# Turning layer 0's memory-head softmax weights: TensorE transposes replaced by VectorE block transposes

## The chip, the cores and the metric

The kernel runs on one core of a Trainium2 chip. The metric is the device time of the program in microseconds (us). The engines named below are TensorE (PE; its weight loads are PEld), VectorE (DVE), ScalarE (ACT), GpSimd (POOL) and SyncE (SP, which issues the DMAs).

## The reference, cut to what matters

A trunk of two decoder layers over 256 tokens of width 2048. Layer 0 mixes tokens by stick-breaking attention, layer 1 by sparse attention; in both, four more heads attend to 256 memory tokens:

```python
def memory_attention(q_mem, mem_n, w_kv):
    km, vm = split_cols(mem_n @ w_kv, [N_MEM_HEADS * HEAD_DIM] * 2)
    ...
    s = jnp.einsum('bthd,bmhd->bhtm', q, km).astype(jnp.float32) * HEAD_DIM ** -0.5
    p = jax.nn.softmax(s, axis=-1)
    return jnp.einsum('bhtm,bmhd->bthd', p.astype(vm.dtype), vm).reshape(...)
```

Each head has head size 128, so `s` and `p` are 256 x 256. The outputs of all 16 heads go through one output projection, then norms, a residual, and a gated feed-forward part with a causal convolution. All is float32.

## The kernel before, in words

**Pieces.** Every large product is cut into pieces: two 128-row slices of a weight matrix by 512 columns, 512 KB. There are 777 pieces, run in one fixed order. A piece is loaded by SP into `raw`, rounded by ACT into `hi` (`round_piece`, L921), and DVE writes the rest into `lo` (`split_piece`, L1194). PE then does 12 matmuls of 128x512 for it (hi by hi, lo by hi, hi by rest; two slices, two token tiles). The buffers form a ring of four (`RING = 4`), and ACT and DVE prepare piece n + 3 at their place n (`LEAD = 3`). PE waits for `lo_done` before each piece; ACT waits until piece n - 1 is finished before it overwrites that piece's `hi` with piece n + 3.

**Ticks.** The number of a piece is the tick. `schedule()` writes a list for each engine: which small steps follow which piece. On PE the steps of tick n come behind the matmuls of piece n; on DVE and ACT the steps of tick n come behind the preparation of piece n + 3. Within a tick they are sorted by `rank`, and steps without a rank of their own (9) stay in the order in which they were entered. Every engine runs its list strictly in that order.

**Memory heads of layer 0.** Heads g = 0 to 3 start at ticks t = 29, 33, 37 and 41 (`at("q0", 5) + 4 * g`):
- tick t, `memA`: PE writes the scores into PSUM bank 4 (four matmuls of 256 columns, `bank<-km,qm`); DVE takes the row maxima (L1361, L1362); ACT takes the exponentials into `pm` (L1068); DVE, `memS`, scales them by the reciprocal sums (L1366, L1368). The DVE steps wait for PE and ACT in turn, and what stands behind them on DVE waits too.
- tick t + 2, `memB`: PE turns `pm` by four 128x128 transposes into bank 6 (L750), ACT copies the bank into `ptm` (L1073).
- tick t + 3, `memC`: PE multiplies the values with `ptm` into bank 5 (four matmuls of 256 columns, `bank<-ptm,vm`), DVE splits the result into `o` (L1372, L1373).

Layer 1's memory heads (g = 4 to 7) use the same functions at later ticks.

**Turning by blocks.** DVE's `transpose` turns 32 x 32 blocks within one instruction. `blocks(k, r)` (L1272) uses it for the projections named in `BY_BLOCKS`: eight instructions of 32 x 256 in a tick, in two ticks. The ones near the memory heads are those of q0 at ticks 34 and 35 and those of k0 at ticks 42 and 43. They were entered into the schedule ahead of the memory heads. The stick-breaking heads begin at tick 46.

Of the kernel before, what the change touches and what calls it, by code (L numbers as in the profile page):

```python
# [23 lines left out]
HEADS, MEM_HEADS, GROUPS = 12, 4, 2  # L24
# [39 lines left out]
class Plan:  # L64
# [20 lines left out]
    def at(self, name, p=-1, off=0):  # L85
        return self.chunks[name].ticks[p] + off

    def do(self, tick, step, *args, on):
        for e in on.split():
            self.steps[e].setdefault(tick, []).append((step, args))  # L90


def schedule():
# [62 lines left out]
    at, do = s.at, s.do  # L156
# [77 lines left out]
    for g in range(MEM_HEADS):  # L234
        t = at("q0", 5) + 4 * g
        do(t, "memA", g, on="pe act dve")
        do(t, "memS", g, on="dve")
        do(t + 2, "memB", g, on="pe act")
        do(t + 3, "memC", g, on="pe dve")
    heads = [at("v0", 6) + 6 * h for h in range(8)] + [at("v2", 6) + 3 * h for h in range(4)]  # L240
    for h, t in enumerate(heads):
        do(t, "stickA", h, on="pe act dve")
# [56 lines left out]
    for g in range(MEM_HEADS):  # L299
        t = [at("qa", 4), at("qa", 6), at("qb", 0), at("qb", 2)][g]  # L300
# [5 lines left out]
    for h in range(HEADS):  # L306
        t = base + 2 * h
# [13 lines left out]


PLAN = schedule()


def build(nc, A):
    with ExitStack() as ctx:
# [3 lines left out]
        def sem(name):  # L331
            return ctx.enter_context(nc.semaphore(name))
# [3 lines left out]
        def region(tensors):  # L336
# [5 lines left out]
        x = sb("x", [P, 2, D])  # L342
        xT, = region([("xT", [P, DT, 2, T], F32)])
        _, y = region([("h_front", [P, DT, T], F32), ("y", [P, 4, 2, W], F32)])
        row_h, mem_a, mem_b = region([("row_h", [P, D], F32), ("mem_a", [P, 4, T], F32), ("mem_b", [P, 4, T], F32)])
        h = sb("h", [P, DT, 2, T], F32R)
# [22 lines left out]
        sb("line", [P, 88])  # L369
        mid, = region([("mid", [P, FT, 2, T], F32R)])  # L370
        _, taps = region([("mid_front", [P, FT - 4, 2, T], F32R), ("taps", [P, 4, W], F32)])
        o, q4, k4 = region([("o", [P, DT, 2, T], F32R), ("q4", [P, 2, 4, T], F32), ("k4", [P, 2, 4, T], F32)])
        _, _, kT, kc, vc = region([
            ("o_a", [P, DT, 2, T], F32R), ("q4_a", [P, 2, 4, T], F32), ("kT", [P, GROUPS, 2, T + 16], F32),
            ("kc", [P, GROUPS, T], F32), ("vc", [P, GROUPS, T], F32)])
# [45 lines left out]
        ms_ready, mb_ready, me_ready, mp_ready, mt_ready, mpt_ready, mv_ready, mo_done = (sem(n) for n in (  # L421
            "ms_ready", "mb_ready", "me_ready", "mp_ready", "mt_ready", "mpt_ready", "mv_ready", "mo_done"))
# [47 lines left out]
        def half(t):  # L470
            return slice(t * P, (t + 1) * P)
# [97 lines left out]
        def _(pe_):  # L569
# [3 lines left out]
            def take(b, by, value):  # L573

                if b in bank_read:
                    pe_.wait_ge(*bank_read[b])
                bank_read[b] = (by, value)
# [165 lines left out]
                m.then_inc(ms_ready, 1)  # L743

            def memB(g):
                take(6, mpt_ready, g + 1)
                pe_.wait_ge(mp_ready, g + 1)
                for m_ in range(2):
                    for t in range(2):
                        m = tr(B[6][:, m_ * T + t * P:m_ * T + (t + 1) * P], pm[:, t, half(m_)], ident)  # L750
                m.then_inc(mt_ready, 1)
# [100 lines left out]
            def nsaC(hd):  # L852
# [5 lines left out]
                if hd == 0:  # L858
# [8 lines left out]

            kinds = {"wide": wide, "gates": gates, "cmp": compress}
            does = {"msum": msum, "turnx": turnx, "turn": turn, "keep_busy": keep_busy, "rxturn": rxturn, "memA": memA, "memB": memB, "memC": memC,
                    "stickA": stickA, "stickB": stickB, "stickC": stickC, "gatesT": gatesT, "hidT": hidT, "cmp": cmp,  # L870
                    "nsaA": nsaA, "nsaB": nsaB, "nsaC": nsaC}
# [16 lines left out]
        def _(act_):  # L888
            act = nc.scalar.activation
# [174 lines left out]

            def memA(g):
                act_.wait_ge(mb_ready, g + 1)
                for t in range(2):
                    act(pm[:, t, :], B[4][:, t * T:(t + 1) * T], ACT.Exp, bias=nb[:, t:t + 1], scale=SCALE,  # L1068
                        accum_out=sums[:, t:t + 1]).then_inc(me_ready, 1)

            def memB(g):
                act_.wait_ge(mt_ready, g + 1)
                act(ptm[:].rearrange("p a t -> p (a t)"), B[6][:, :], ACT.Copy).then_inc(mpt_ready, 1)  # L1073

            def stickA(hd):
# [68 lines left out]
            def nsaB(hd):  # L1144
                act_.wait_ge(nt_ready, 2 * hd + 1)
                act(pts[:], B[6][:, :], ACT.Copy).then_inc(npt_act, 1)  # L1146

            does = {"feed_mem": feed_mem, "msum": msum, "feed_x": feed_x, "turnx": turnx, "mem_square": mem_square, "xsq": xsq, "xscale": xscale, "rx": rx_root, "evac": evac,
                    "keep": keep, "ychunk": ychunk, "warm": warm, "tile": tile, "last_tile": last_tile, "post": post, "memA": memA, "memB": memB,
                    "stickA": stickA, "stickB": stickB, "silu": silu, "midhi": midhi, "angles": angles,  # L1150
                    "gates": gates, "gatesT": gatesT, "windows": windows, "hidden": hidden, "hidT": hidT,
# [8 lines left out]
        def _(dve):  # L1160
# [4 lines left out]
            def finish(ins):  # L1165
                ins.then_inc(dve_step, 1)
                count[0] += 1
                dve.wait_ge(dve_step, count[0])
# [195 lines left out]
            def memS(g):  # L1364
# [3 lines left out]
                    m = ts(pm[:, t, :], pm[:, t, :], rs[:, t:t + 1], None, ALU.mult)  # L1368
                m.then_inc(mp_ready, 1)

            def split_out(k, src, by):
                finish(ts(o[:, k, 0, :], src, 1.0, None, ALU.mult))  # L1372
                tt(o[:, k, 1, :], src, o[:, k, 0, :].bitcast(F32), ALU.subtract).then_inc(by, 1)  # L1373

            def memC(g):
                dve.wait_ge(mv_ready, g + 1)
                split_out(HEADS + g % MEM_HEADS, B[5][:, 0:T], mo_done)
# [9 lines left out]
            def stickC(hd):  # L1387
                dve.wait_ge(pv_ready, hd + 1)
                split_out(hd, B[5][:, 0:T], ho_done)
# [129 lines left out]
            def nsaC(hd):  # L1519
                dve.wait_ge(pv_ready, HEADS + hd + 1)  # L1520
                split_out(hd, B[4][:, 0:T], ho_done)

            does = {"feed_mem": feed_mem, "msum": msum, "feed_x": feed_x, "turnx": turnx, "rx": rx_inverse, "turned": turned_copy, "blocks": blocks,
                    "rope": rope, "ychunk": ychunk, "post": post, "xadd": xadd, "tile": tile, "last_tile": last_tile, "mem_square": mem_square, "memA": memA, "memS": memS, "memC": memC, "stickA": stickA,
                    "stickC": stickC, "conv": conv, "rxturn": rxturn, "turnmid": turnmid, "gateup": gateup, "midlo": midlo, "gatesT": gatesT,
                    "windows": windows, "hidT": hidT, "cmp": cmp, "nsaA": nsaA, "nsaS": nsaS, "nsaB": nsaB, "nsaC": nsaC}
            for n in range(-LEAD, TICKS):
# [121 lines left out]
```

## Time and profile before

| | |
|---|---|
| time, median of 3 runs | 2240.47 us (2240.29 to 2240.64) |
| the profiled execution's own time | 2240.5 us |
| its span | 2238.6 us |
| granted TensorE clock, mean | 0.999 of 2.4 GHz |
| busy: PE, DVE, ACT | 2227.5, 1594.8, 1151.7 us |
| DMA | 459 MB, mean 205 GB/s |

The span is the stretch that the profile covers; the remaining 1.9 us of the time lie around it. Busy time is the time in which an engine had an instruction in flight. In the timeline view a line gives the start of an instruction (or of a run of equal ones), its length, engine, line of the kernel, operation, tiles and shapes, and how many instructions it stands for; brackets hold idle time of the engine before it and what ended that.

### The profile page before, as it was taken

What the parts mean: (1) busy time and instruction counts of PE and PEld (TensorE: products, weight loads), DVE (VectorE), ACT (ScalarE), POOL (GpSimd) and SP (SyncE); (2) the same over time, 40 slices, a digit from 0 to 9 for tenths busy, and PEclk for the clock granted to TensorE, in tenths of its full rate; (3) what the DMA queues carried; (4) which work ended last, traced back from release to release, by engine and by line L of the source; (5) the groups of instructions that cost most, each with busy time, mean ns of one, the idle gap of its engine ahead of it and who ended that gap; (6) DMA issues with size and microseconds to landing.
All of it is one profiled execution on the core that took longest, in us unless ns stands there. A gap on an engine that the chain in (4) does not pass through costs nothing.

```text
span 2238.6 us, 26396 instructions
## 1 busy us (share of the span) xinstructions
PE 2227.5 (100%) x10172; PEld 1838.7 (82%) x10172; DVE 1594.8 (71%) x2163; ACT 1151.7 (51%) x1558; POOL 18.7 (1%) x20
## 2 busy tenths in 40 slices
PE   9999999999999999999999999999999999999998
PEld 7888888888888888888888887788888888888887
DVE  7777675788888888544566678757888888784444
ACT  7556674654454544444574554456544454544443
POOL 0000000000000000000030000000000000000000
PEclk9999999999999999999999999999999999999999
DMA  9554555677776777676655843356776777766664
GB/s 329 182 172 155 180 174 191 206 229 224 237 233 224 233 227 236 196 228 196 194 179 178 270 141 104 123 179 189 245 237 224 234 222 238 237 215 205 191 196 150
DMA packets 128285, 459.00 MB, mean 205 GB/s; under 512 B 14784, under 2 KB 17088, under 8 KB 127392
## 3 DMA queue, kind: packets, MB, share of 16 engines
q1 hardware_dynamic: 127888, 456.78, 63.3%
q8 instruction: 81, 1.33, 0.2%
q0 software_dynamic: 128, 0.48, 0.1%
q14 instruction: 44, 0.36, 0.0%
q10 hardware_dynamic: 144, 0.05, 0.0%
HBM read 443.71 MB, written 2.10 MB: 199 GB/s over the span
## 4 chain that ended last, share of the span: by engine, by line
PE 98%; DVE 1%; ACT 0%; DMA 0%; issue 0%; SPq 0%; DVEq 0%; ACTq 0%
PE bank L580 97%; PE bank L703 0%; DVE lo L1194 0%; PE bank L717 0%; DMA raw<-in_mem 0%; DVE x L1324 0%; PE bank L750 0%; PE bank L842 0%; PE bank L849 0%; ACT h L964 0%; DVE x L1357 0%; ACT mf L1038 0%; DVE y L1320 0%; DVE h L1232 0%; ACT root L1040 0%
## 5 line engine op out<-in xcount | busy, mean ns | idle before, releaser
L1194 DVE TENSOR_TENSOR lo<-raw,hi 128x1024 fp32r<-128x1024 f32 x776 | 945.1, 1223 | 511.1 <-ACT hi L921 504.9
L580 PE MATMUL bank<-hi,h 128*128 128x512 f32 x3904 | 1226.9, 392 | 0.4 <-ACT h L964 0.4
L921 ACT ACTIVATE hi<-raw 128x1024 fp32r<-128x1024 f32 x776 | 817.1, 1058 | 785.9 <-PE bank L580 756.6
L580 PEld LDWEIGHTS bank<-hi,h 128*128 128x128 f32 x3904 | 732.9, 188 | 151.7 <-issue 0.9
L580 PE MATMUL bank<-lo,h 128*128 128x512 f32 x1952 | 760.1, 389 | 0.0
L580 PE MATMUL bank<-hi,mid 128*128 128x512 f32 x1408 | 434.0, 389 | 0.0
L580 PEld LDWEIGHTS bank<-lo,h 128*128 128x128 f32 x1952 | 366.7, 188 | 74.1
L580 PEld LDWEIGHTS bank<-hi,mid 128*128 128x128 f32 x1408 | 264.3, 188 | 55.1
L580 PE MATMUL bank<-lo,mid 128*128 128x512 f32 x704 | 273.9, 389 | 0.0
L580 PE MATMUL bank<-hi,o 128*128 128x512 f32 x512 | 163.8, 394 | 0.0
L1437 DVE STREAM_TRANSPOSE cv<-mf 32x256 f32<-32x256 f32 x352 | 154.0, 437 | 6.4
L580 PEld LDWEIGHTS bank<-lo,mid 128*128 128x128 f32 x704 | 132.1, 188 | 27.2
L580 PEld LDWEIGHTS bank<-hi,o 128*128 128x128 f32 x512 | 96.2, 188 | 19.5
L580 PE MATMUL bank<-lo,o 128*128 128x512 f32 x256 | 99.8, 390 | 0.0
L580 PE MATMUL bank<-hi,amem 128*128 128x512 f32 x256 | 83.1, 397 | 1.0 <-DVE amem L1174 0.6
L580 PEld LDWEIGHTS bank<-hi,amem 128*128 128x128 f32 x256 | 48.5, 189 | 12.2 <-DVE lo L1184 1.0
L1096 ACT ACTIVATE mid<-cv 128x512 fp32r<-128x512 f32 x44 | 25.4, 625 | 60.6 <-DVE cv L1437 60.6
L1001 ACT ACTIVATE st<-bank,rxp 128x512 f32<-128x512 f32 x88 | 54.9, 674 | 3.2 <-PE bank L580 3.2
L580 PEld LDWEIGHTS bank<-lo,o 128*128 128x128 f32 x256 | 48.1, 188 | 9.5
L580 PE MATMUL bank<-lo,amem 128*128 128x512 f32 x128 | 50.1, 392 | 0.0
L1146 ACT ACTIVATE pts<-bank 128x512 f32<-128x512 f32 x12 | 7.2, 597 | 48.6 <-PE bank L844 48.6
L1447 DVE TENSOR_TENSOR mid<-cv,mid 128x512 fp32r<-128x512 f32 x44 | 28.3, 684 | 0.0
(231 smaller groups left out, 1213.5 us busy)
## 6 DMA issues: line engine op xcount, KB each, us to landing
raw<-in_gate SPq DMA_DIRECT2D x176, 512.0 KB, 4.2
raw<-in_up SPq DMA_DIRECT2D x176, 512.0 KB, 3.6
raw<-in_down SPq DMA_DIRECT2D x176, 512.0 KB, 4.2
raw<-in_in SPq DMA_DIRECT2D x136, 512.0 KB, 4.1
raw<-in_out SPq DMA_DIRECT2D x64, 512.0 KB, 3.9
taps<-in_taps SPq DMA_DIRECT2D x44, 512.0 KB, 5.4
raw<-in_mem SPq DMA_DIRECT2D x31, 512.0 KB, 4.2
st<-st SPq DMA_DIRECT2D x22, 448.0 KB
```

Source lines behind the costliest of these rows:

```text
L580: return mm(out, lhsT, rhs, start=first, stop=last, skip_group_check=True)
L921: act(hi[k][:, 0:w], raw[k][:, 0:w], ACT.Copy).then_inc(hi_done, 1)
L1001: act(st[:, k % 2, t, :], B[c.banks[t]][:, :], ACT.Copy, scale=scale_of(scale)[:, t:t + 1])\
L1096: act(mid[:, kt:kt + 2, 0, :], cv[:, b, :].rearrange("p (q t) -> p q t", q=2), ACT.Copy)\
L1146: act(pts[:], B[6][:, :], ACT.Copy).then_inc(npt_act, 1)
L1194: tt(lo[k][:, 0:w], raw[k][:, 0:w], hi[k][:, 0:w].bitcast(F32), ALU.subtract).then_inc(lo_done, 1)
L1437: m = nc.vector.transpose(turned_[32 * r:32 * r + 32, :, :, 32 * a:32 * a + 32], made[32 * a:32 * a + 32, :, :, r, :])
L1447: tt(mid[:, kt:kt + 2, 1, :], cv[:, b, :].rearrange("p (q t) -> p q t", q=2), mid[:, kt:kt + 2, 0, :].bitcast(F32), ALU.subtract).then_inc ...
```

## The change

The turn of layer 0's weights leaves PE and ACT. A new DVE step `memR(g, r)` writes `ptm` straight from `pm`: 16 transposes of 32 partitions by 128 elements (2 x 2 x 32) for a head, eight at tick t + 1 (r = 0) and eight at t + 2 (r = 1). `memC` moves from t + 3 to t + 4, which is the tick of the next head's `memA`; `memC` has the lower rank and comes first. `memR` has no rank of its own and is entered behind `blocks`. `memR` waits for the scaled `pm` and for the product of the head before (which reads `ptm`); ACT's `memA` waits until the head before has been turned, since its exponentials overwrite `pm`. Layer 1's heads keep `memB`; its ACT wait counts from the fourth head.

```diff
-        do(t + 2, "memB", g, on="pe act")
-        do(t + 3, "memC", g, on="pe dve")
+        for r in range(2):
+            do(t + 1 + r, "memR", g, r, on="dve")
+        do(t + 4, "memC", g, on="pe dve")
...
             def memA(g):
                 act_.wait_ge(mb_ready, g + 1)
+                if 0 < g < MEM_HEADS:
+                    act_.wait_ge(mpt_ready, g)
...
             def memB(g):
-                act_.wait_ge(mt_ready, g + 1)
+                act_.wait_ge(mt_ready, g - MEM_HEADS + 1)
...
+            def memR(g, r):
+
+                dve.wait_ge(mp_ready, g + 1)
+                if g:
+                    dve.wait_ge(mv_ready, g)
+                made = pm[:].rearrange("p t (k b i) -> p t k b i", k=2, i=32)
+                to = ptm[:].rearrange("p k (t m) -> p t k m", t=2)
+                for b in (2 * r, 2 * r + 1):
+                    for a in range(4):
+                        m = nc.vector.transpose(to[32 * b:32 * b + 32, :, :, 32 * a:32 * a + 32],
+                                                made[32 * a:32 * a + 32, :, :, b, :])
+                if r:
+                    m.then_inc(mpt_ready, 1)
```

## Rows read from the trace of the kernel before

**Rows 1.** The page: busy time of each engine, and the chain that ended last by line.
```profile
PE 2227.5 (100%) x10172; PEld 1838.7 (82%) x10172; DVE 1594.8 (71%) x2163; ACT 1151.7 (51%) x1558; POOL 18.7 (1%) x20
...
PE bank L580 97%; PE bank L703 0%; DVE lo L1194 0%; PE bank L717 0%; DMA raw<-in_mem 0%; DVE x L1324 0%; PE bank L750 0%; PE bank L842 0%; PE bank L849 0%; ACT h L964 0%; DVE x L1357 0%; ACT mf L1038 0%; DVE y L1320 0%; DVE h L1232 0%; ACT root L1040 0%
```

**Rows 2.** Waits of PE over the whole span: total us, times, longest.
```profile
PE bank L580 <- DVE st L1171: 1.5, 1, 1.5
PE bank L703 <- DVE x L1324: 0.6, 2, 0.3
PE bank L580 <- DVE amem L1174: 0.6, 1, 0.6
PE bank L580 <- DVE lo L1194: 0.5, 1, 0.5
PE bank L580 <- ACT h L964: 0.4, 2, 0.2
```

**Rows 3.** Timeline of PE around head 0's turn and product.
```profile
97.49 0.39 PE L580 MATMUL bank<-lo,h 128*128 128x512 f32 x1
97.72 0.39 PE L580 MATMUL bank<-hi,h 128*128 128x512 f32 x1
97.95 0.60 PE L750 MATMUL bank<-cst,pm 128*128 128x128 f32 x4
98.62 0.39 PE L580 MATMUL bank<-lo,h 128*128 128x512 f32 x1
101.14 1.02 PE L580 MATMUL bank<-ptm,vm 128*128 128x256 f32 x4
102.23 0.40 PE L580 MATMUL bank<-lo,h 128*128 128x512 f32 x1
104.77 1.02 PE L580 MATMUL bank<-km,qm 128*128 128x256 f32 x4
117.97 1.02 PE L580 MATMUL bank<-km,qm 128*128 128x256 f32 x4
```

**Rows 4.** Timeline of ACT at head 0's turn.
```profile
98.58 0.60 ACT L1073 ACTIVATE ptm<-bank 128x512 f32<-128x512 f32 x1 [2.04 <-PE bank L750]
```

**Rows 5.** Timeline of DVE from head 0's weights to head 1's maxima.
```profile
95.59 2.36 DVE L1194 TENSOR_TENSOR lo<-raw,hi 128x1024 fp32r<-128x1024 f32 x2
101.32 1.23 DVE L1194 TENSOR_TENSOR lo<-raw,hi 128x1024 fp32r<-128x1024 f32 x1 [3.37 <-ACT hi L921]
102.46 0.42 DVE L1372 TENSOR_SCALAR o<-bank 128x256 fp32r<-128x256 f32 x1
103.25 1.22 DVE L1194 TENSOR_TENSOR lo<-raw,hi 128x1024 fp32r<-128x1024 f32 x1
105.84 0.69 DVE L1361 TENSOR_REDUCE mxs<-bank 128x2 f32<-128x512 f32 x1 [1.37 <-PE bank L580]
```

**Rows 6.** Timeline of DVE from head 1's weights to head 2's maxima.
```profile
108.77 1.23 DVE L1194 TENSOR_TENSOR lo<-raw,hi 128x1024 fp32r<-128x1024 f32 x1
109.92 3.56 DVE L1272 STREAM_TRANSPOSE q<-st 32x256 f32<-32x256 f32 x8
118.39 1.23 DVE L1194 TENSOR_TENSOR lo<-raw,hi 128x1024 fp32r<-128x1024 f32 x1
121.46 0.68 DVE L1361 TENSOR_REDUCE mxs<-bank 128x2 f32<-128x512 f32 x1
```

**Rows 7.** DVE groups by line and shape: count, busy us, mean ns.
```profile
L1272 DVE STREAM_TRANSPOSE q<-st 32x256 f32<-32x256 f32 x48 | 20.9, 436 | 0.7
L1512 DVE TENSOR_SCALAR ps<-ps,wgt 128x256 f32<-128x256 f32 x24 | 7.3, 347 | 0.0
L1512 DVE TENSOR_SCALAR ps<-ps,wgt 128x128 f32<-128x128 f32 x24 | 5.7, 280 | 0.0
L1291 DVE TENSOR_TENSOR st<-ropeD 128x256 f32<-128x256 f32 x18 | 7.7, 425 | 0.6
L1289 DVE TENSOR_TENSOR ropeD<-st,sinf 128x128 f32<-128x128 f32 x18 | 5.1, 283 | 0.0
```

**Rows 8.** Timeline of PE: its first matmuls, and its last.
```profile
1.47 4.63 PE L580 MATMUL bank<-st 128*128 128x256 f32 x10 [1.47 <-DVE st L1171]
6.33 0.63 PE L580 MATMUL bank<-lo,amem 128*128 128x512 f32 x1
7.39 0.40 PE L580 MATMUL bank<-lo,amem 128*128 128x512 f32 x1
...
2230.94 0.39 PE L580 MATMUL bank<-hi,mid 128*128 128x512 f32 x1
```

**Rows 9.** Stretches at the end: length, busy of five engines, granted clock, DMA.
```profile
2232.00:2236.00 4.00, 0.00 (x0) 0.00 (x0) 3.46 (x8) 2.46 (x6) 0.00 (x0) 1.00 0.30 117
2236.10:2238.60 2.50, 0.00 (x0) 0.00 (x0) 0.04 (x1) 0.00 (x0) 0.00 (x0) 0.50 0.70 270
```

More of the change, by code:

```diff
@@ L1523, in _ @@
             does = {"feed_mem": feed_mem, "msum": msum, "feed_x": feed_x, "turnx": turnx, "rx": rx_inverse, "turned": turned_copy, "blocks": blocks,
-                    "rope": rope, "ychunk": ychunk, "post": post, "xadd": xadd, "tile": tile, "last_tile": last_tile, "mem_square": mem_square, "memA": memA, "memS": memS, "memC": memC, "stickA": stickA,
+                    "rope": rope, "ychunk": ychunk, "post": post, "xadd": xadd, "tile": tile, "last_tile": last_tile, "mem_square": mem_square, "memA": memA, "memS": memS, "memR": memR, "memC": memC, "stickA": stickA,
                     "stickC": stickC, "conv": conv, "rxturn": rxturn, "turnmid": turnmid, "gateup": gateup, "midlo": midlo, "gatesT": gatesT,
```

## The prediction

> **What bounds the kernel now.** I read the page first: PE is busy for 2227.5 of 2238.6 us and the chain that ended last runs through the matmuls of the pieces (line 580) for 97% of the span, while DVE has 29% of idle time [rows 1]. Then the waits of PE: five kinds, together 3.6 us in the whole span, all at the start or at the norms [rows 2]. None lies near the memory heads. So in the stretch of the change PE runs without a gap: whatever leaves PE there comes off the time, and whatever PE waits there is added to it. Nothing later gives a delay back, since no later wait of PE exists in which it could vanish. The question is therefore read from two timelines, PE's and DVE's, between 90 and 150 us: when does DVE have `ptm` ready, and when does PE ask for it?
>
> **What PE saves.** Neighbouring matmuls of 512 columns start 0.23 us apart (97.49, 97.72). From the start of head 0's transposes to the second matmul behind them are 0.67 us (97.95 to 98.62); one matmul lies between, so the turn costs PE 0.67 - 0.23 = 0.44 us [rows 3]. Four heads: 1.76 us saved. Behind the turn a piece takes 101.14 - 97.95 - 0.44 = 2.75 us, and the product costs PE 102.23 - 101.14 - 0.23 = 0.86 us [rows 3]. It is moved, not changed. ACT loses a 0.60 us copy and a wait of 2.04 us [rows 4]; it had that time idle, so this is worth nothing. ACT's new wait falls behind `mb_ready`, which DVE gives later in its own list than the turn it asks for: free. Behind it stands the rounding of the next pieces, but it never decides. DVE's wait for the product before is free too: PE does that product ahead of the scores that DVE has already used. The shifted count of layer 1's `memB`, and the DMAs, cost nothing: no transfer is added or moved, and loads stay behind the ring.
>
> **What one turn costs on DVE.** No row shows a transpose of 32x128. The existing ones of 32x256 take 436 ns, and eight in a row 3.56 us, so they start (3.56 - 0.44) / 7 = 0.446 us apart [rows 6, 7]. With 128 instead of 256 elements a tensor_tensor falls from 425 to 283 ns (by 142), a tensor_scalar from 347 to 280 (by 67) [rows 7]. The transpose's 436 ns is nearest to the tensor_tensor, so I take 0.446 - 0.142 = 0.30 us; the bounds are half the price, 0.22, and the whole, 0.446. A portion of eight is then 2.4 us (1.8 to 3.6), a head 4.8 us, four heads 19.4 us of new DVE work in place of 1.8 us of PE work.
>
> The Trainium skill, page "VectorE: DVE Perf Modes", section "Rules for kernel authors", advises against this exchange: for a 128x128 transpose TensorE, if its destination may be PSUM. Its section "The three transpose paths" has 390 ns for TensorE's (bf16). Four of them a head would make the saving an estimated 6.2 us; the trace has them 0.44 us together [rows 3], a quarter of that, so the measured 1.76 us stands in the sum.
>
> **Where it lies, head by head.** Times are those of the old trace, moved.
>
> Head 0 (ticks 29 to 33). DVE begins the preparation behind the weights at 95.59: two pieces in 2.36 us, and 3.37 us idle before the next [rows 5]. With two portions between, `ptm` is ready at 95.59 + 2.36 + 4.8 = 102.75. PE wants it one piece later than before and without the turn: 101.14 - 0.44 + 2.75 = 103.45. Hidden, with 0.7 us to spare. DVE then has two pieces (2.36) and the split of the product (0.79, from 102.46 to 103.25 [rows 5]), and is free at 105.9; head 1's maxima, at 105.84 before, start about there.
>
> Head 1 (ticks 33 to 37) is where it breaks. Ticks 34 and 35 already hold 16 transposes of q0. From maxima to the end of the weights are 2.93 us (105.84 to 108.77); then two pieces and 16 transposes take 9.62 us (108.77 to 118.39) [rows 5, 6]. The portions come behind the q0 transposes of their ticks and add 4.8: ready at 105.9 + 2.93 + 9.62 + 4.8 = 123.25. PE wants it just before head 2's scores: 117.97 - 2 x 0.44 - 0.86 = 116.2 [rows 3]. PE stands for 7.0 us. The preparation of the pieces does not decide here: PE still has the prepared piece 38.
>
> Head 2 (ticks 37 to 41) has no other transposes. DVE runs on from 123.25 with two pieces and the split, 3.07 us (118.39 to 121.46 [rows 6]), maxima to weights 2.93, two pieces 2.36 and two portions 4.8: ready at 136.4. PE wants it one round later. A round was 117.97 - 104.77 = 13.20, less 0.44 is 12.76 [rows 3]: 136.0. A stall of 0.4 us.
>
> Head 3 (ticks 41 to 45) meets k0's transposes, as head 1 met q0's: 136.4 + 3.07 + 2.93 + 9.62 + 4.8 = 156.8, wanted at 136.4 + 12.76 = 149.2. A stall of 7.6 us. Afterwards DVE is one tick ahead of the first stick-breaking head and has caught up.
>
> Stalls 7.0 + 0.4 + 7.6 = 15.0, less 1.8: +13.2 us at an undisturbed clock.
>
> **The clock.** PE has never stood for more than 1.5 us [rows 2], so the trace has no stall of 7 us. But it shows the clock at the edges. PE's last matmul starts at 2230.94 and takes 0.39; the granted clock is still 1.00 up to 2236.0 and 0.50 (1.2 GHz) behind it: it fell 4.7 us after PE had stopped [rows 8, 9]. At the start PE's matmuls were slow from 1.47 us on (0.63 us at 6.33) and at full pace at 7.39 (0.40) [rows 8]: up to 5.3 us of work at half the clock, which costs up to 2.6 us. Two stalls are longer than 4.7 us. I take that the clock falls in both and that each costs 2.6 us (bounds 0 and 2.6). The slow stretch behind stall 1 also lets DVE catch up: head 2's stall vanishes and PE, 2.2 us later at head 3's product than without it, waits there about 6.5 instead of 7.6. The sum: 7.0 + 2.6 + 6.5 + 2.6 - 1.8 = +16.9 us. The profiled execution's 2240.5 (span 2238.6 and 1.9 around it; the median of the runs is 2240.47, the same) becomes 2257.4.
>
> The Trainium skill says the same of the clock in "TensorE: Matmul & The Clock Gate", in the rules at its end (idle gaps between bursts bring the half rate back); no row of this case shows it within a kernel.
>
> **Bounds.** With 1.8 us a portion head 1's turn is ready at 121.55 and the stalls are 5.3 and 5.7: +9.2, 2249.7 us without a fall of the clock. With 3.6 us head 0 stalls too (1.7), then 10.1, 2.8 and 10.1: +23 us, 2263.5, with the clock up to 2268.
>
> **The rivals.**
> 1. The stalls come, the clock holds. For it: it held for more than 4 us after the last matmul, and the two stalls pass that only by 2 to 3 us. Against it: they do pass it. 2240.5 + 13.2 = 2253.7.
> 2. The other side: DVE hides the turn and only PE's 1.8 us remain: 2238.7, no measurable change. For it: DVE is 29% idle, and in head 0 its idle 3.37 us and the added tick suffice. It would need to have head 1's `ptm` ready by 116.2. But even transposes of no length would leave it at 105.4 + 2.93 + 9.62 = 117.95, because q0's come first: with nothing for the turn there are still two stalls of 1.7 us, +1.6 in all. The change is within 0.2% (4.5 us, what a measurement of this kernel can tell) only if a portion costs under 0.7 us, 90 ns a transpose. Nothing in the rows is near that.
> 3. The 32x128 transposes cost as much as the 32x256 (a fixed cost per instruction, or the broken-up pattern): 2263 to 2268. Against it: every other shape pair gets cheaper with its length.
>
> **How the numbers follow.** Forecast (stalls and clock) 0.55, rival 1 0.24, rival 3 0.12, rival 2 or something close to it 0.07, a case not seen, with a gain, 0.02. The predicted time is 2257. The range takes in the low price and rival 1, and most of rival 3: 2249 to 2265. Faster by over 0.2% 0.02, within it 0.07, slower by more 0.91.
>
> **What would show it.** The new transposes, 64 of them, at about 300 ns. PE with two long waits for DVE's `ptm` ahead of the products of heads 1 and 3, near 116 and 150 us, of about 7 us each, none for head 0, and at most a short one for head 2. No transposes of PE and no copy of ACT near 98 us. A granted clock of 0.50 for a few us behind each long wait, with matmuls of over 0.5 us. Everything from about 170 us on as before, only later. I am wrong if the transposes take under 200 ns, if PE's waits are for `lo` and not for `ptm`, or if no wait over 3 us is there.

## The result and the profile after

The changed kernel takes 2258.79 us (median of 5 runs, 2257.79 to 2259.04) against 2240.47 us: the ratio is 1.0081, 95% interval 1.0066 to 1.0096. It is 18.3 us slower. Forecast were 2257 us, from two stalls of TensorE and two falls of its clock; that is what happened.

The page of the kernel after, busy time (answers to [rows 1]):

```profile
PE 2230.5 (99%) x10156; PEld 1840.6 (82%) x10156; DVE 1614.8 (72%) x2227; ACT 1150.5 (51%) x1554; POOL 18.8 (1%) x20
```

PE's work is almost the same, DVE has 20.0 us more, and the span grew by 17.9 us (2238.6 to 2256.5). So PE waits. Its waits over the whole span (answers to [rows 2]):

```profile
PE bank L581 <- DVE ptm L1384: 14.6, 2, 7.7
PE bank L581 <- DVE st L1175: 1.5, 1, 1.5
PE bank L581 <- DVE lo L1198: 0.8, 1, 0.8
```

The first line is new: two waits for the turned weights, written by the new transposes (L1384). The others lie where they lay before, at the start of the program and at the norms. The timeline of PE shows them with their surroundings (answers to [rows 3]):

```profile
103.40 1.02 PE L581 MATMUL bank<-ptm,vm 128*128 128x256 f32 x4
104.26 1.03 PE L581 MATMUL bank<-km,qm 128*128 128x256 f32 x4
115.79 0.39 PE L581 MATMUL bank<-hi,h 128*128 128x512 f32 x1
123.89 2.05 PE L581 MATMUL bank<-ptm,vm 128*128 128x256 f32 x4 [7.71 <-DVE ptm L1384]
125.72 1.91 PE L581 MATMUL bank<-km,qm 128*128 128x256 f32 x4
...
139.35 1.02 PE L581 MATMUL bank<-ptm,vm 128*128 128x256 f32 x4
...
151.74 0.39 PE L581 MATMUL bank<-hi,h 128*128 128x512 f32 x1
159.02 2.05 PE L581 MATMUL bank<-ptm,vm 128*128 128x256 f32 x4 [6.89 <-DVE ptm L1384]
...
164.93 0.81 PE L581 MATMUL bank<-q,k 128*128 128x256 f32 x4
```

The products of heads 0 and 2 (103.40, 139.35) come without a wait, those of heads 1 and 3 do not. The four matmuls of a product take 1.02 us in the one case and 2.05 in the other: behind each wait the clock is at half. DVE's timeline from head 0's weights to head 1's turned weights (answers to [rows 5, 6]):

```profile
95.60 1.23 DVE L1198 TENSOR_TENSOR lo<-raw,hi 128x1024 fp32r<-128x1024 f32 x1
96.75 2.49 DVE L1384 STREAM_TRANSPOSE ptm<-pm 32x128 f32<-32x128 f32 x8
99.25 1.23 DVE L1198 TENSOR_TENSOR lo<-raw,hi 128x1024 fp32r<-128x1024 f32 x1
100.51 2.53 DVE L1384 STREAM_TRANSPOSE ptm<-pm 32x128 f32<-32x128 f32 x8
...
110.20 3.57 DVE L1276 STREAM_TRANSPOSE q<-st 32x256 f32<-32x256 f32 x8
113.78 2.51 DVE L1384 STREAM_TRANSPOSE ptm<-pm 32x128 f32<-32x128 f32 x8
116.31 1.23 DVE L1198 TENSOR_TENSOR lo<-raw,hi 128x1024 fp32r<-128x1024 f32 x1
117.56 3.61 DVE L1276 STREAM_TRANSPOSE q<-st 32x256 f32<-32x256 f32 x8
121.21 2.53 DVE L1384 STREAM_TRANSPOSE ptm<-pm 32x128 f32<-32x128 f32 x8
```

Read it downwards: at 116.0 us, when PE wants head 1's turned weights, DVE is at the end of the first of two portions, and a piece and eight of q0's transposes stand ahead of the other. Last the clock, in stretches cut at the ends of the waits and of the slow parts (columns: length, busy time of PE, PEld, DVE, ACT, POOL, granted clock, DMA):

```profile
116.20:119.30 3.10, 0.00 (x0) 0.00 (x0) 3.01 (x6) 0.00 (x0) 0.00 (x0) 1.00 0.24 38
119.30:123.80 4.50, 0.00 (x0) 0.00 (x0) 4.27 (x14) 0.00 (x0) 0.00 (x0) 0.50 0.23 90
123.90:129.50 5.60, 5.60 (x13) 4.47 (x14) 3.85 (x6) 0.90 (x4) 0.00 (x0) 0.50 0.54 187
129.60:146.00 16.40, 16.40 (x74) 13.64 (x73) 14.58 (x33) 8.23 (x13) 0.00 (x0) 1.00 0.39 130
...
152.00:156.80 4.80, 0.13 (x1) 0.00 (x0) 4.61 (x11) 1.06 (x1) 0.00 (x0) 1.00 0.37 109
156.90:159.00 2.10, 0.00 (x0) 0.01 (x1) 1.99 (x8) 0.00 (x0) 0.00 (x0) 0.50 0.00 0
159.00:163.60 4.60, 4.58 (x11) 3.66 (x12) 4.16 (x5) 0.00 (x0) 0.00 (x0) 0.50 0.48 151
```

The bill, from the starts of PE's matmuls. The last matmul before a wait starts 0.23 us before PE could go on.

- Wait at head 1: 123.89 - 115.79 - 0.23 = 7.9 us.
- Clock behind it: from this product to the next are 139.35 - 123.89 = 15.5 us. The same round at full clock takes 115.79 + 0.23 - 103.40 = 12.6 us in this trace, so 2.8 are for the clock.
- Wait at head 3: 159.02 - 151.74 - 0.23 = 7.1 us.
- Clock behind it: from this product to the first stick-breaking scores are 164.93 - 159.02 = 5.9 us in place of 0.86 + 2.75, so 2.3 are for the clock.

Together 20.1. Those scores start 17.8 us later than in the kernel before (164.93 against the line below), and the span grew by 17.9, so PE saved 2.3 us elsewhere. The four turns are 1.8 of it; the rest is the round, 12.6 us where 13.20 less 0.44 makes 12.76.

```profile
147.14 0.81 PE L580 MATMUL bank<-q,k 128*128 128x256 f32 x4
```

### The profile page after: what moved, and what is told of

Same layout as the page of the kernel before. It is cut to its first block, busy times and chain, and to the rows that moved or that the text cites. A ratio compares the mean times of both kernels' runs of the same rounds, so it can differ in the third digit from the quotient of the medians.

```text
span 2256.5 us, 26429 instructions
## 1 busy us (share of the span) xinstructions
PE 2230.5 (99%) x10156; PEld 1840.6 (82%) x10156; DVE 1614.8 (72%) x2227; ACT 1150.5 (51%) x1554; POOL 18.8 (1%) x20
## 4 chain that ended last, share of the span: by engine, by line
PE 94%; DVE 4%; ACT 1%; issue 0%; DMA 0%; SPq 0%; DVEq 0%; ACTq 0%
PE bank L581 93%; DVE lo L1198 1%; DVE ptm L1384 1%; PE bank L704 0%; ACT hi L923 0%; DVE km L1276 0%; DVE qm L1276 0%; PE bank L718 0%; DVE q L1276 0%; DVE k L1276 0%; DMA raw<-in_mem 0%; DVE x L1328 0%; ACT pm L1072 0%; PE bank L844 0%; ACT h L966 0%
```

## The experiments

The theory: each turn has a due time on PE; DVE's list is strict and has no room from head 0 to head 3, so its work there becomes waits of PE, and long waits cost the clock as well. The rivals differ from one run to the next. The kernel before, run beside them, was between 2240.55 and 2240.72 us.

**Which heads do it.** Heads 1 and 3 turned by DVE, 0 and 2 by PE; then the other way round. The edit, with `BY_DVE` as (1, 3) or (0, 2):

```diff
-        for r in range(2):
-            do(t + 1 + r, "memR", g, r, on="dve")
-        do(t + 4, "memC", g, on="pe dve")
+        if g in BY_DVE:
+            for r in range(2):
+                do(t + 1 + r, "memR", g, r, on="dve")
+        else:
+            do(t + 2, "memB", g, on="pe act")
+        do(t + (4 if g in BY_DVE else 3), "memC", g, on="pe dve")
```

> Heads 1 and 3 (whose turns share ticks with the turns of q0 and k0) are turned by VectorE, heads 0 and 2 by TensorE as before the change. Theory (each turn has a due time on TensorE, and only the two heads that meet 16 other transposes miss it): two stalls of about 6.9 us with two falls of the clock, 2.8 and 2.3 us, less 0.9 for two turns saved: 2258.5 us, the whole loss with half of the turns. Rival (the loss is the sum of VectorE work added, 4.8 us a head): half of the loss, about 2249.5 us.

> The other half: heads 0 and 2 by VectorE, heads 1 and 3 by TensorE. Theory: head 0 hidden as in the changed kernel; head 2's scores are reached late by VectorE (it still works off q0's transposes and head 1), so its turn would end about 131.9 us against a due time of 129.5: one wait of 2.4 us, less 0.9 saved: 2242 us, no fall of the clock. Rival (sum of added work): about 2249.5. A pure collision account, without the backlog, would give 2239.6.

Heads 1 and 3: 2257.81 us (ratio 1.0077, 1.0061 to 1.0092), two waits of 6.9 us. Half of the turns bring practically the whole loss; the rival of an equal share a head falls. The half-clock time left behind the waits was shorter than in the changed kernel:

```profile
123.50:127.60 4.10, 4.10 (x10) 3.29 (x11) 3.31 (x5) 0.00 (x0) 0.00 (x0) 0.50 0.43 130
...
158.40:161.70 3.30, 3.27 (x8) 2.65 (x9) 3.27 (x5) 0.00 (x0) 0.00 (x0) 0.50 0.29 66
```

Half of each is lost, an estimated 2.1 and 1.7 us, where the changed kernel lost 2.8 and 2.3.

Heads 0 and 2: 2244.15 us (1.0015, 1.0006 to 1.0025), 2 us above what was expected. PE and the stretches of this kernel, at head 2:

```profile
132.79 1.88 PE L587 MATMUL bank<-ptm,vm 128*128 128x256 f32 x4 [2.91 <-DVE ptm L1390]
```

```profile
129.60:132.70 3.10, 0.28 (x2) 0.00 (x0) 2.94 (x10) 0.00 (x0) 0.00 (x0) 1.00 0.52 126
132.70:136.00 3.30, 3.21 (x9) 2.62 (x9) 3.10 (x4) 0.00 (x0) 0.00 (x0) 0.54 0.41 101
136.00:140.00 4.00, 4.00 (x18) 3.27 (x18) 2.30 (x6) 2.66 (x6) 0.00 (x0) 0.95 0.60 217
```

The wait is there, 2.9 us for the expected 2.4. What the expectation missed is the clock: after no more than this idle time it ran at half for 3.4 us, worth 1.7. So head 2 can be late although no other transposes stand in its ticks and heads 1 and 3 bring no new ones: DVE's backlog from q0 is enough.

**What the clock costs.** Matmuls of no use ahead of the two waits:

```diff
+        if g % 2:
+            do(t + 4, "keep_busy", 56 if g == 1 else 68, on="pe")
         do(t + 4, "memC", g, on="pe dve")
...
-    rank = {"nsaB": 0,
+    rank = {"keep_busy": -1, "nsaB": 0,
```

> The changed kernel with matmuls of no use (56 and 68 of 128x256, about 0.12 us each) on TensorE ahead of the waits of heads 1 and 3, so that it is idle for under 2 us in each. Theory: the clock stays full. The second wait is then longer by what the slow stretch had hidden, since VectorE has no idle time between the two: the gain is only the second slow stretch and VectorE's one wait, 2.3 + 0.8 us: 2255.7 us. Rival (each fall of the clock simply adds its 2.3 to 2.8 us): 2253.7 us. If the clock had nothing to do with it: 2259.

Measured: 2255.22 us (1.0065, 1.005 to 1.008), 3.6 us less than the changed kernel (the two sets of runs do not overlap). PE and the stretch of the second wait:

```profile
137.28 1.10 PE L583 MATMUL bank<-ptm,vm 128*128 128x256 f32 x4 [0.59 <-DVE ptm L1386]
...
150.02 8.31 PE L583 MATMUL bank<-neg 128*128 128x256 f32 x68
158.17 1.02 PE L583 MATMUL bank<-ptm,vm 128*128 128x256 f32 x4
```

```profile
150.00:158.20 8.20, 8.20 (x70) 8.18 (x69) 7.87 (x20) 1.06 (x1) 0.00 (x0) 1.00 0.22 66
```

The clock stays full, and the product of head 3 still starts only at 158.17, 8.15 us after PE could have had it (7.1 in the changed kernel). The matmuls of no use are not what holds it up: DVE ends the turned weights at 157.84 (155.31 + 2.53), 0.3 us before. Head 2 waits too, for 0.6 us. The first slow stretch had been time in which DVE caught up; without it PE waits instead. Of the 5.1 us that the slow clock took, 3.6 were a real loss.

**Whether DVE's order matters.** The memory heads' transposes ahead of those of q0 and k0 in the same ticks:

```diff
-    rank = {"nsaB": 0,
+    rank = {"memR": 8, "nsaB": 0,
```

> The changed kernel with the memory heads' transposes ranked ahead of q0's and k0's in their ticks. All VectorE work is the same. Theory (VectorE has no spare time from head 1 to head 3, so its order moves the waits and only partly removes them): heads 1, 2 and 3 each wait about 4.2 us, 12.6 in all, less 1.8: 2251 us if the clock holds, up to 2256 if it falls. Rival (only the collision in the tick counts): waits of 4.2 us at heads 1 and 3 and none at head 2, 2247 us. Rival (the order is of no account): 2259.

Measured: 2254.64 us (1.0061, 1.0046 to 1.0076). Three waits now, at heads 1, 2 and 3:

```profile
119.80 1.21 PE L581 MATMUL bank<-ptm,vm 128*128 128x256 f32 x4 [4.06 <-DVE ptm L1384]
...
136.91 1.25 PE L581 MATMUL bank<-ptm,vm 128*128 128x256 f32 x4 [2.60 <-DVE ptm L1384]
...
154.01 1.28 PE L581 MATMUL bank<-ptm,vm 128*128 128x256 f32 x4 [2.56 <-DVE ptm L1384]
```

Head 2, which had no wait, has one, so the collision in a tick is not all. The clock fell 0.8 us behind the start of each product, when the wait was already over, and each time it ran at half for 3.4 us. The first stretch from the product on:

```profile
119.80:126.00 6.20, 6.20 (x21) 5.03 (x22) 6.06 (x11) 0.00 (x0) 0.00 (x0) 0.72 0.08 19
```

The later waits are shorter than the 4.2 us expected; that the slowed PE met DVE halfway fits this, but no run with this order and a kept clock shows it.

**DVE's old work out of the way.** q0 and k0 turned by PE instead:

```diff
-BY_BLOCKS = ["mem0k", "qm0"] + [f"{n}{i}" for i in range(3) for n in "qk"]
+BY_BLOCKS = ["mem0k", "qm0"] + [f"{n}{i}" for i in range(1, 3) for n in "qk"]
```

> The changed kernel, but q0 and k0 are turned by TensorE (16 transposes of 128x128 each, about 1.9 us, and two copies of 0.68 us on VectorE in place of 16 transposes, 7.2 us). VectorE loses 5.8 us of work ahead of heads 1 and 3. Theory: the waits shrink to under 1 us each, the clock holds: 2240.5 - 1.8 + 3.8 + 0.7 = 2243.2 us. Rival (the new transposes are harmful without the old ones beside them): above 2250 us.

Measured: 2243.11 us (1.0011, 1.0002 to 1.002). PE waits for `ptm` three times, 0.9 us at the most, and the clock holds. With 5.8 us less on DVE ahead of heads 1 and 3 the new transposes do no harm; PE pays for the 32 turns.

**A later due time.** Each product at t + 5:

```diff
-        do(t + 4, "memC", g, on="pe dve")
+        do(t + 5, "memC", g, on="pe dve")
```

> The changed kernel with each product one tick later still (t + 5, behind the next head's scores). Theory (VectorE is full from head 0 to head 3, so a later due time helps once, not at each head): the second wait becomes partly a wait for lo, since VectorE is behind with the pieces; one piece of 2.75 us is gained in all, and about 2 us more from shorter slow stretches: 2251 to 2256 us, best estimate 2254. Rival (each late head has 2.75 us more): 5.5 us less in waits and hardly a fall of the clock, 2249 us or below, no waits for lo.

Measured: 2252.89 us (1.0057, 1.0043 to 1.007). The waits of this kernel:

```profile
PE bank L581 <- DVE lo L1198: 5.5, 3, 4.3
PE bank L581 <- DVE ptm L1384: 4.1, 2, 3.3
```

0.8 us of the first line lie at the start of the program, so between 84 and 170 us PE waits 8.8 us in all where it waited 14.6. A wait of 4.3 us for `lo` has taken the place of the second wait for `ptm`. The later due time gained 5.9 us in all, where one piece once (2.75) and about 2 us from shorter slow stretches were expected. What is left of the second wait has only changed its name, as one expects of a DVE that is behind.

**DVE's work doubled.** Each portion's transposes done twice:

```diff
+                for again in range(2):
                     for b in (2 * r, 2 * r + 1):
                         for a in range(4):
...
+                    if not again:
+                        finish(m)
```

> The changed kernel with every new transpose done twice (same result), 5.0 us more of VectorE work a head. Theory (once head 0 has lost its 0.4 us of slack, VectorE is full and each us of its work is a us of the program): 4 x 5.0 less under 1 us of its idle time, +19 us: 2278 us, with waits for ptm at all four heads. Rival (only heads 1 and 3 are late, the others have room): +10 us, 2269 us.

Measured: 2280.02 us (1.0174, 1.0161 to 1.0188), 21.2 us over the changed kernel for 19.9 us of DVE's busy time (1634.7 for 1614.8), with four waits of 4.6, 11.3, 3.8 and 12.0 us. In this stretch a microsecond more of DVE is about a microsecond more of the program.

**Where DVE has room.** The last four kernels ask whether the turn on DVE can pay at all. Four portions of four transposes, and ticks set head by head; first:

```diff
-        t = at("q0", 5) + 4 * g
+        t = (29, 37, 50, 62)[g]
...
+        for r in range(4):
+            do(t + ((1, 2, 3, 4) if g < 2 else (1, 3, 4, 5))[r], "memR", g, r, on="dve")
+        do(t + (6, 8, 8, 8)[g], "memC", g, on="pe dve")
```

> All four heads still turned by VectorE, but placed where it has room: heads at ticks 29, 37, 50 and 62, the turn in four portions of four transposes in four ticks, the product 6 to 8 ticks behind the scores. Theory (the loss is one of due times in a crowded stretch, the gain of 0.44 us a head on TensorE is real): no wait for ptm, 1.76 us less than before: 2238.7 us. Rival (the transposes slow VectorE's preparation of the pieces wherever they stand): at or above 2240.5 us, with waits for lo.

Measured: 2243.23 us (1.0011, 1.0002 to 1.002): missed. Three heads were hidden; head 3's portions met k1's transposes (ticks 66 and 67), its product waited 2.3 us, and the clock fell for 3.4:

```profile
221.64 2.05 PE L581 MATMUL bank<-ptm,vm 128*128 128x256 f32 x4 [2.33 <-DVE ptm L1383]
```

So head 3's portions went to ticks 63, 65, 68 and 69, its product to 74; with it a control, the kernel before with its heads at these four ticks and PE's turns (`t = (29, 37, 50, 62)[g]`):

> As the spread kernel, which still had one wait of 2.3 us: head 3's four portions met k1's 16 transposes at ticks 66 and 67. Here its portions stand at ticks 63, 65, 68 and 69 and its product at 74. Theory: no wait for ptm and none for lo near 220 us, full clock, 1.76 us less than before: 2238.8 us. Rival (the loss follows the new transposes wherever they stand): still above 2240.5.

> Control: the kernel before with its four memory heads at ticks 29, 37, 50 and 62, turned by TensorE. Theory (the placement alone is worth nothing, TensorE had no wait there): 2240.5 us, so that any difference to the spread kernel with VectorE's turns is the price of the turn on TensorE, 1.76 us. Rival (the placement is what helps): as fast as the spread kernel.

The spread kernel: 2241.4 us (1.0003, 0.9994 to 1.0011), missed again by 2.6 us. No wait for `ptm` is left, but these:

```profile
PE bank L581 <- DVE spl L1402: 1.9, 2, 1.5
...
PE bank L581 <- DVE lo L1198: 1.5, 2, 1.3
```

`spl` is what DVE hands to a stick-breaking head. The longer wait ends at 227.65; DVE's list shows two portions of the turn just ahead of that head's steps:

```profile
220.41 1.26 DVE L1383 STREAM_TRANSPOSE ptm<-pm 32x128 f32<-32x128 f32 x4
221.68 1.23 DVE L1198 TENSOR_TENSOR lo<-raw,hi 128x1024 fp32r<-128x1024 f32 x1
222.94 1.26 DVE L1383 STREAM_TRANSPOSE ptm<-pm 32x128 f32<-32x128 f32 x4
```

The shorter, at 187.51, comes behind the split of head 2's product and eight of q1's transposes, and not behind a portion. Of the waits for `lo` the one of 1.3 us lies at the start of the program, ahead of every change; the other is 0.2 us. The control: 2240.52 us (1.0, 0.9991 to 1.0009), so the placement itself is worth nothing. In the last kernel head 3 moved to tick 74, and head 2's last portion and product moved back to ticks 61 and 63, away from those two stick-breaking heads:

```diff
-        t = (29, 37, 50, 62)[g]
+        t = (29, 37, 50, 74)[g]
...
-            do(t + ((1, 2, 3, 4), (1, 2, 3, 4), (1, 3, 4, 5), (1, 3, 6, 7))[g][r], "memR", g, r, on="dve")
-        do(t + (6, 8, 8, 12)[g], "memC", g, on="pe dve")
+            do(t + ((1, 2, 3, 4), (1, 2, 3, 4), (1, 3, 4, 11), (1, 3, 4, 5))[g][r], "memR", g, r, on="dve")
+        do(t + (6, 8, 13, 8)[g], "memC", g, on="pe dve")
```

> The spread kernel again, clear of every crowded tick: scores at ticks 29, 37, 50 and 74; head 2's portions at 51, 53, 54 and 61 and its product at 63; head 3's portions at 75, 77, 78 and 79 and its product at 82. The last spread kernel lost 2.4 us in three small waits, two of them because portions delayed VectorE's part of a stick-breaking head near 188 and 227 us. Theory: none of these waits is left and TensorE's 1.76 us show: 2238.8 us, 0.08% faster than before. Rival (some other small wait takes their place, VectorE has no room for 19.7 us more without one): 2240 us or more.

Measured: 2239.31 us, 11 runs from 2238.71 to 2239.76, beside 15 of the kernel before from 2240.17 to 2240.98. The ratio is 0.9994 (0.9985 to 1.0003): the two sets of runs do not overlap, but the interval takes in 1, so no gain is claimed beyond what the trace shows. Its PE waits from 84 to 400 us:

```profile
PE bank L581 <- DVE spl L1402: 0.4, 1, 0.4
PE bank L704 <- DVE x L1328: 0.3, 1, 0.3
PE bank L581 <- ACT h L966: 0.2, 1, 0.2
PE bank L704 <- DVE x L1361: 0.2, 1, 0.2
```

The middle two are there in the kernel before as well. New are 0.4 and 0.2 us; 1.76 less 0.6 is 1.2, and the medians differ by 1.2. The agreement is closer than it deserves: PE's waits in the first 84 us, ahead of every change, come to 2.6 us in the profile of the kernel before, 2.0 in this one and 3.2 in the spread kernel ahead of it.

## Why the prediction was right

- *PE saves 0.44 us a head.* Held, as far as the bill resolves it, and again in the last kernel. In the changed kernel a little more is saved, 2.3 us in all: with the product directly ahead of the scores the round is 12.6 us, where 12.76 was predicted.
- *A transpose of 32x128 costs 0.30 us.* The 64 of them took 303 ns each, eight in a row 2.49 to 2.53 us (predicted 2.4). The step from the existing 32x256 (436 ns) by the difference of the tensor_tensor pair was the right one; both bounds were far off.
- *Head 0 hidden, with 0.7 us to spare.* Ready at 103.04 (100.51 + 2.53), the product at 103.40 without a wait: 0.4 to spare.
- *Head 1 stalls 7.0 us.* 7.9. Ready at 123.74, predicted 123.25; wanted at 116.0, predicted 116.2. Ready came 0.5 us late, by the portions of 2.5 us; PE asked 0.2 earlier, by the shorter round, and started 0.15 after ready.
- *No stall at head 2 once the clock has fallen; 6.5 us at head 3.* None, and 7.1. The working of the 6.5 does not hold: its own terms are 7.6 less the 2.2 us by which PE comes later, and that is 5.4. DVE was in fact 2.1 us later than the working had it (ready at 158.87, not 156.8): 0.8 in its wait for PE's slow scores and 0.9 in its eight portions are the larger part. That the step came out near was partly luck; with 5.4 the sum is 2256.3.
- *The stalls without the clock: 7.0, 0.4 and 7.6 us.* The kernel with kept clock shows them: 7.9, 0.6 and 8.15.
- *The clock falls in both, 2.6 us each.* It fell in both, for 2.8 and 2.3 us. Rival 1 (it holds, 2253.7) was wrong about the clock. Its time was 1.5 us below that of the kernel with kept clock (2255.2). That the fall came was reasoned; its price was near by luck. It was taken from the start of the program, where the matmuls were slow for up to 5.3 us (read from their lengths; the clock column shows 1.00 there). What is left of the half clock behind a wait differs: 5.6 and 4.7 us in the changed kernel, 4.1 and 3.3 in the one that turns only heads 1 and 3. The prediction had taken 4.7 us after the last matmul as the point to pass. The clock fell 3.1 us after the last matmul ended in the first wait and 4.7 in the second, and in five later kernels it fell around each of the nine waits of 2.3 to 4.6 us. So the edge row gave the right answer for these long waits, but no safe limit for shorter ones: the expectation for heads 0 and 2 went wrong there, and the one for the order turned round had to leave the clock open.
- *The other side (DVE hides it).* Excluded by the row that was used: q0's transposes alone pass the due time. Only by emptying that stretch or leaving it does the turn on DVE become free.
- What the prediction had only half said: it worked through the backlog head by head but spoke of two collisions. The runs with the order turned round, with a later due time and with doubled work show that the stretch as a whole is full. In the changed kernel DVE is busy for 57.0 of the 63.3 us from 95.6 to 158.9. Of the rest it waits for PE only once, for 0.8 us, and three times for ACT's exponentials, 3.3 us in all, which stand in its own chain.

## What to carry to other kernels

When work moves from the engine that bounds the kernel to one that is 70% busy, do the sum on that engine's own timeline for the stretch in question, with everything that stands ahead of the moved work in its list, and compare the moment it is ready with the moment it is wanted. Here 1.8 us were to be had, and the 16 VectorE transposes of a head cost 5 us. In a full stretch that comes back as waits, and every wait of 2.3 us or more in these runs brought half-clock time with it. If it is to pay, spread it in small portions over ticks without other work, and let the consumer come many ticks later; here even that was worth 1.2 us of 2240.

## What the runs showed of the hardware

- TensorE's clock fell to 1.2 GHz in waits of 7 and 8 us, and also around all nine waits of 2.3 to 4.6 us. It stayed at 2.4 GHz through waits of up to 1.5 us, and with matmuls of no use in a wait of 8 us. Around the waits of 2.3 to 4.1 us the half clock lasted 3.4 us each time, an estimated 1.7 us of loss where PE worked all through it. With DVE's order turned round (waits of 2.6 to 4.1 us) it began 0.8 us after the wait was over.
- Slow TensorE time is not simply added to the waits: the engine that was late uses it to catch up (5.1 us lost, 3.6 given back when the clock was kept).
- VectorE's transposes in float32: 32x256 436 ns, 32x128 303 ns, in a row 0.31 us apart. Half the elements, in a more broken-up pattern, take 30% less. Four TensorE transposes of 128x128 in the stream of matmuls cost 0.44 us against 16 x 0.31 = 5.0 us on VectorE.
